# The ten products of each merge stage, each made of seven products of quarters

## The reference, cut to what matters

```python
for l in range(DEPTH):                      # DEPTH = 2
    h = rmsnorm(x, norm_w[l])               # x: 256 x 1024
    proj = h @ w_in[l]
    (..., gate_a, gate_b) = jnp.split(proj, SPLIT_IDX, axis=-1)
    y_a = gated_delta_branch(...)           # 256 x 1024
    y_b = diff_attention_branch(...)        # 256 x 1024
    merged = (jax.nn.sigmoid(gate_a) * (y_a @ w_pa[l])
              + jax.nn.sigmoid(gate_b) * (y_b @ w_pb[l]))
    x = x + merged @ w_out[l]
```

## Time and profile before

| | |
|---|---|
| time, three runs | 2027.78 us median, 2026.0 to 2027.93 |
| profiled execution | 2026.38 us, its span 2024.6 us |
| merge stage of layer 0, first gate product to turning of x | 330.83 to 477.21 us of the span |
| TensorE, VectorE, ScalarE, GpSimd busy | 1957.6, 747.8, 421.5, 100.1 us |

### The profile page before, as it was taken

One profiled execution on the slowest core, in us unless ns is written; L12 is line 12 of the kernel. 1 busy time (PEld: TensorE's weight loads), 2 busy tenths in 40 slices (PEclk: granted clock), 3 DMA queues, 4 the chain that ended last, 5 costly groups with the idle time before them and its releaser, 6 DMA issues.

```text
span 2024.6 us, 26469 instructions
## 1 busy us (share of the span) xinstructions
PE 1957.6 (97%) x10820; PEld 1052.1 (52%) x10820; DVE 747.8 (37%) x2088; ACT 421.5 (21%) x1076; POOL 100.1 (5%) x84
## 2 busy tenths in 40 slices
PE   8999999999999999999999999999999999999997
PEld 7854667886854567884553333333333333333334
DVE  4868675213759676211242122221122112111213
ACT  2261564111061565211131000000000000000003
POOL 0031220000021220000000000000000000000000
PEclk9999999999999999999999999999999999999999
DMA  7634122343643212347659999999999999999992
GB/s 264 252 122 164 46 84 84 126 156 136 226 144 130 84 43 85 125 171 261 227 216 393 428 427 427 429 430 428 431 427 432 430 426 431 429 429 427 428 422 89
DMA packets 99843, 552.29 MB, mean 273 GB/s; under 512 B 8685, under 2 KB 15249, under 8 KB 78738
## 3 DMA queue, kind: packets, MB, share of 16 engines
q1 hardware_dynamic: 99730, 550.66, 67.5%
HBM read 547.43 MB, written 3.21 MB: 272 GB/s over the span
## 4 chain that ended last, share of the span: by engine, by line
PE 81%; DMA 15%; ACT 1%; DVE 1%; SPq 1%; issue 1%; DVEq 0%; ACTq 0%
PE bank L652 29%; DMA region<-w_gate_up_dram 15%; PE bank L1236 14%; PE bank L1268 8%; PE bank L774 6%; PE bank L1010 3%; PE bank L995 3%; PE bank L1179 2%; PE bank L1165 2%; PE bank L1094 1%; PE bank L1223 1%; PE bank L854 1%; PE bank L911 1%; SPq L457 1%; PE bank L878 1%
## 5 line engine op out<-in xcount | busy, mean ns | idle before, releaser
L652 PE MATMUL bank<-region 128*128 128x256 f32 (+2 forms) x2352 | 604.2, 417 | 4.9 <-DVE region L1734 2.6
L652 PEld LDWEIGHTS bank<-region 128*128 128x128 f32 x2352 | 439.8, 190 | 157.9 <-issue 106.5
L1236 PE MATMUL bank<-region 128*64 128x512 f32 x1872 | 416.6, 598 | 22.5 <-DMA region<-w_gate_up_dram 21.6
L1236 PEld LDWEIGHTS bank<-region 128*64 128x64 f32 x1872 | 131.2, 138 | 303.8 <-issue 263.6
L2346 DVE TENSOR_SCALAR region<-bank 128x512 f32<-128x512 f32 x32 | 22.1, 692 | 681.7 <-PE bank L1236 681.7
L1268 PE MATMUL bank<-region 128*64 128x512 f32 x944 | 210.6, 597 | 9.5 <-issue 8.1
L1268 PEld LDWEIGHTS bank<-region 128*64 128x64 f32 x944 | 77.4, 137 | 123.3 <-issue 123.3
L774 PE MATMUL bank<-region 128*128 128x512 f32 x256 | 129.2, 607 | 0.0
L1679 ACT ACTIVATE region<-region 128x512 f32<-128x512 f32 x32 | 20.2, 630 | 512.6 <-DVE region L2346 512.6
L1683 ACT ACTIVATE region<-bank 128x512 f32<-128x512 f32 x32 | 19.1, 597 | 326.9 <-PE bank L1268 326.9
L1840 DVE SCALAR_TENSOR_TENSOR region<-region,layer_mem 128x256 f32<-128x256 f32 x192 | 78.0, 477 | 0.0
(11 more groups left out here) (348 smaller groups left out, 1929.4 us busy)
## 6 DMA issues: line engine op xcount, KB each, us to landing
region<-w_gate_up_dram SPq DMA_DIRECT2D x32, 4096.0 KB, 38.9
region<-w_down_dram SPq DMA_DIRECT2D x59, 2048.0 KB, 34.5
region<-w_gate_up_dram SPq DMA_DIRECT2D x53, 2048.0 KB, 21.6
region<-w_in_dram SPq DMA_DIRECT2D x43, 2048.0 KB, 8.4
layer_mem<-w_gate_up_dram SPq DMA_DIRECT2D x11, 2048.0 KB, 35.4
region<-w_out_dram SPq DMA_DIRECT2D x6, 2048.0 KB, 8.0
layer_mem<-w_down_dram SPq DMA_DIRECT2D x5, 2048.0 KB, 36.4
region<-rows_scratch SPq DMA_DIRECT2D x4, 2048.0 KB, 9.3
```

The source lines that it names most:

```text
L652: mm = pe.matmul(dst, lhs(k), w(k), start=(k == 0), stop=(k == n_k - 1))
L1236: mm = pe.matmul(pb[g][hf * 64:(hf + 1) * 64, :], XT[:, 2 * (j % 2) + kk, j // 2, :], wj[:, kk, c:c + NB], start=(first and j == 0 and kk ...
```

## The change

Each tile's product, 256 positions by 1024 by 512, is cut in two along each side. With the halves of the 1024 rows called k0, k1, of the 512 columns f0, f1, of the positions t0, t1, seven products of quarters (128 positions, 512 rows, 256 columns) take the place of the eight that the plain form has. Sums of quarters stand in for quarters, and results are carried from one quarter of the output to the next:

- GpSimd makes four sums or differences of weight quarters for each tile (`tile_sums`), each 128 partitions by 1024 elements. Three go to memory of their own, one overwrites a quarter of the tile. Tile 0's come behind the diagonal of head 6, tile 1's behind that of head 7, tile 2's and 3's wait for all gating, the later ones for product 6 of two tiles before, and the last of the four for its product 3. Each operation but the third waits for the one that it reads.
- VectorE makes four sums of row quarters (`row_sum`), 128x512 each, for hT (in heads 2 to 5), yaT, ybT and mT.
- TensorE adds up products in PSUM quarters of 256 columns. A product of tiles 0 to 7 is two blocks of 128 features, four matmuls of 128 positions each; in tiles 8 and 9 it is four matmuls of 256 columns. Each ends with a signal of its own, counted in `MERGE_ORDER`.
- ScalarE copies one PSUM quarter into another twice per tile (`upper_right`, `lower_left`), so that TensorE adds on top.
- VectorE takes a tile's quarters out as they get ready (`on_upper`, `lower_right`, then `gate_lower` or `gate_merge`), and keeps the gate's scaling, clamp and multiplication.
- Turned rows of y_a and y_b (and of x from layer 1 on) go to banks 0, 1, 2, 4; products 4 and 3 of tile 1 stand between the turnings and the wait for their copies.
- Slots are freed by product 3 of their tile. The loads of the mixing stage's first tiles wait for product 3 of tiles 0, 1 and 7 of layer 1 instead of all gating.
- Some single signals share a semaphore, two groups of matmuls in the heads (`attention_out`, `chunk_out`) mark their start once per bank, and a fill of zeros is wider.

The core of the diff:

```diff
+        def w_quarter(w, f, kh):
+            return w[:, kh * 4:kh * 4 + 4, f * S:(f + 1) * S]
+        def row_quarter(rows_T, kh, t):
+            return rows_T[:, kh * 4:kh * 4 + 4, t * P:(t + 1) * P]
...
+        MERGE_ORDER = ((1, 0), (5, 0), (2, 0), (6, 0), (1, 1), (7, 0), (2, 1), (5, 1), (6, 1), (4, 0), (3, 0), (7, 1), (4, 1), (3, 1),
+                       (1, 2), (5, 2), (2, 2), (6, 2), *((p, i - (p in (7, 4, 3))) for i in range(3, 8) for p in (1, 5, 7, 2, 6, 4, 3)),
+                       (1, 8), (7, 7), (5, 8), (4, 7), (3, 7), (1, 9), (5, 9), *((p, i) for p in (2, 6, 7, 4, 3) for i in (8, 9)))
...
-            if pos < 24:
-                return "merge_ps1", l * 8 + pos - 15
-            return "xo_ps", l * 4 + pos - 21
+            return "product_ps", products_until(l, 3, pos - 16)
...
+                def quarter(p, i, weights, rows_of, f, t, start=False):
+                    dst = quarter_ps(i, f, t)
+                    if i >= 8:
+                        for k in range(4):
+                            mm = pe.matmul(dst, rows_of[:, k, :], weights[:, k, :], start=(start and k == 0), stop=(k == 3), skip_group_check=True)
+                        mm.then_inc(s("product_ps"), 1)
+                        return
+                    for b in range(2):
+                        for k in range(4):
+                            mm = pe.matmul(dst[:, b, :], weights[:, k, b * P:(b + 1) * P], rows_of[:, k, :],
+                                           start=(start and b == 0 and k == 0), stop=(k == 3), skip_group_check=True)
+                    mm.then_inc(s("product_ps"), 1)
...
+                product_1(0)
+                product_5(0)
                 chunk_state(H - 1)
-                gate_part(0, 0, 0, 1)
+                product_2(0)
+                product_6(0)
                 chunk_ws(H - 1)
-                gate_part(0, 0, 1, 0)
+                product_1(1)
                 chunk_out(H - 1)
+                product_7(0)
+                product_2(1)
+                pe.wait_ge(s("gd_qs"), hb + H)
+                product_5(1)
...
+                transpose16(lambda t, k: ya[:, k, t, :], 3 * l + 1, bank=ROW_BANKS, between=lambda: product_4(1))
                 pe.wait_ge(s("z_gated"), l * 8 + 8)
+                transpose16(blk(qb), 3 * l + 2, bank=ROW_BANKS, between=lambda: product_3(1))
+                product_1(2)
...
+                for i in range(3, 8):
+                    product_1(i)
+                    product_5(i)
+                    product_7(i - 1)
+                    product_2(i)
+                    product_6(i)
+                    product_4(i - 1)
+                    product_3(i - 1)
+                product_1(8)
+                product_7(7)
+                product_5(8)
+                product_4(7)
+                product_3(7)
+                product_1(9)
+                product_5(9)
+                for product_of in (product_2, product_6, product_7, product_4, product_3):
+                    product_of(8)
+                    product_of(9)
...
+                def upper_right(i):
...
+                    act.wait_ge(s("product_ps"), products_until(l, 1, i))
+                    act.activation(quarter_ps(i, 0, 1), quarter_ps(i, 0, 0), ACT.Copy).then_inc(s("quarter_cp"), 1)
...
+                    if 2 <= n < 6:
+                        row_sum(hT, hT_sum, n - 2, 0)
...
+                def lower_right(i):
+                    dve.wait_ge(s("product_ps"), products_until(l, 7, i))
+                    dve.tensor_tensor(right_quarter(i, 1), right_quarter(i, 0), quarter_ps(i, 1, 0), ALU.add).then_inc(s("w_c3"), 1)
...
+                def gate_merge(i):
+                    g, m = i // 4, i % 2
+                    dve.wait_ge(s("product_ps"), products_until(l, 3, i))
+                    dve.wait_ge(s("w_c3"), l * MERGED + i + 1)
+                    in_layer.do(dve.tensor_tensor(gate_quarter(1, m, 0), gate_quarter(1, m, 0), quarter_ps(i, 1, 0), ALU.mult))
+                    dve.tensor_tensor(right_quarter(i, 0), right_quarter(i, 0), quarter_ps(i, 0, 1), ALU.add).then_inc(s("quarter_out"), 1)
+                    dve.wait_ge(s("quarter_out"), quarters_out(l, "lower", i))
+                    for f in range(2):
+                        in_layer.do(dve.tensor_tensor(gate_quarter(f, m, 1), gate_quarter(f, m, 1), right_quarter(i, f), ALU.mult))
...
+                    if m == 1:
+                        for f in range(2):
+                            dve.tensor_tensor(mT[:, 4 * g + 2 * f:4 * g + 2 * f + 2, :], mg[2 * f].rearrange("p (b c) -> p b c", b=2),
+                                              mg[2 * f + 1].rearrange("p (b c) -> p b c", b=2), ALU.add).then_inc(s("merged"), 1)
...
+                gate_clamp(0)
+                copies16(3 * l + 1, lambda k: (yaT[:, k, :], None), ROW_BANKS)
...
+                for n in range(4):
+                    row_sum(yaT, yaT_sum, n, 4)
+                copies16(3 * l + 2, lambda k: (ybT[:, k, :], None), ROW_BANKS)
...
+                def tile_sums(i):
...
+                    pool.wait_ge(s(f"w_in_slot{slot}"), 16 * (k + 1))
+                    pool.tensor_tensor(sums[:, 0], w_quarter(w, 1, 0), w_quarter(w, 1, 1), ALU.add).then_inc(s("w_sum"), 1)
+                    pool.wait_ge(s("w_sum"), 4 * T + 1)
+                    pool.tensor_tensor(sums[:, 1], sums[:, 0], w_quarter(w, 0, 0), ALU.subtract).then_inc(s("w_sum"), 1)
+                    pool.tensor_tensor(w_quarter(w, 1, 0), w_quarter(w, 0, 0), w_quarter(w, 1, 0), ALU.subtract).then_inc(s("w_sum"), 1)
+                    pool.wait_ge(s("w_sum"), 4 * T + 2)
+                    if i >= 4:
+                        pool.wait_ge(s("product_ps"), products_until(l, 3, i - 2))
+                    pool.tensor_tensor(sums[:, 2], w_quarter(w, 0, 1), sums[:, 1], ALU.subtract).then_inc(s("w_sum"), 1)
...
                     diagonal(n)
+                    if n == H - 2:
+                        tile_sums(0)
+                for i in range(1, MERGED):
+                    tile_sums(i)
```

More of the change, by code:

```diff
@@ L712, in _ @@
                         pe.wait_ge(s("const_in"), 16 * 9)
-                        pe.wait_ge(s("rel_wide"), 1)
-                        pe.matmul(pb[4][:, :], rel_wide, bucket, start=True, stop=True).then_inc(s("bias_ps"), 1)
+                        await_once(pe, "rel_wide")
+                        pe.matmul(pb[4][:, :], rel_wide, bucket, start=True, stop=True).then_inc(once("bias_ps"), 1)
                     if u == 2:
@@ L911, in chunk_out @@
                             mm = pe.matmul(pb[7][:, t * P:(t + 1) * P], E_all[:, n, 2 * d + t, :], us[:, 2 * d + t, :],
-                                           start=(d == 0), stop=(d == 1))
+                                           start=(t == 0 and d == 0), stop=(d == 1), skip_group_check=True)
                     mm.then_inc(s("gd_o_ps"), 1)
@@ L2172, in gate_clamp @@
+                def gate_clamp(i):
+                    m = i % 2
+                    dve.wait_ge(s("quarter_out"), quarters_out(l, "lower", i))
+                    for f in range(2):
+                        in_layer.do(dve.tensor_tensor(gate_quarter(f, m, 1), gate_quarter(f, m, 1), rr_rows(1), ALU.mult))
                     in_layer.fence()
-                    for m in range(2):
-                        ins = dve.tensor_scalar(mg[2 * j + m], mg[2 * j + m], -40.0, None, ALU.max)
+                    for f in range(2):
+                        ins = dve.tensor_scalar(mg[2 * f + m], mg[2 * f + m], -40.0, None, ALU.max)
+                        if f == 0:
+                            in_layer.do(ins)
@@ new lines, in _ @@
+                gate_clamp(1)
+                dve.wait_ge(s("tr_act"), 2 * (3 * l + 3))
+                dve.wait_ge(s("tr_dve"), 2 * (3 * l + 3))
+                for n in range(4):
+                    row_sum(ybT, ybT_sum, n, 8)
+                on_upper(2)
+                lower_right(2)
+                on_upper(3)
+                gate_merge(2)
+                lower_right(3)
+                gate_merge(3)
+                dve.wait_ge(s("merged"), 4 * l + 2)
+                on_upper(4)
@@ new lines, in _ @@
+                lower_right(4)
+                row_sum(mT, mT_sum, 0, 12)
+                on_upper(5)
+                gate_lower(4)
+                gate_clamp(4)
+                lower_right(5)
+                on_upper(6)
+                gate_lower(5)
+                gate_clamp(5)
+                lower_right(6)
+                on_upper(7)
+                gate_merge(6)
+                lower_right(7)
+                gate_merge(7)
+                dve.wait_ge(s("merged"), 4 * l + 4)
+                for n in range(1, 4):
+                    row_sum(mT, mT_sum, n, 12)
@@ new lines, in x_quarter, with x_add @@
+                def x_quarter(i, f, t):
+                    c = (i - 8) * NB + f * S
+                    return x[:, t, c:c + S]
+                def x_add(i, f, t, src):
```

(8 more changed lines are left out.)

312 lines of the change are left out of this document (204 added, 108 removed).

## The result

Changed kernel: 2062.15 us median of 4 runs (2060.81 to 2064.43); kernel before on the same chip: 2027.86 us, 4 runs (2026.0 to 2028.35). The ratio is 1.0172, 95% interval 1.0154 to 1.0190: slower by 1.7%, 34.3 us. The forecast was 2047. The profiled execution has a span of 2059.0 us, against 2024.6 of the earlier trace rows.

What follows compares the result with a forecast made beforehand. TensorE's matmul stream bounds the merge. Per layer, 129.3 us of TensorE work plus 26.9 idle from VectorE waiting for GpSimd, less 146.4, gives +9.8; 2026.4 + 2 x 9.8 = 2046.0, stated as 2047 us against the median, range 2003 to 2066.

Steps and rivals of the forecast that it cites:

- likeliest case: Whole kernel: GpSimd's operation takes between 2.3 and 2.5 us, giving 2040 to 2053 us; chance 0.42.
- C: TensorE's clock falls to half pace behind new gaps, 1.8 us lost six times, 11 more: 2058 us; chance 0.15.
- ceiling: Merge: TensorE alone, with some 0.7 us of idle, would save at most 16.4 us per layer, 33 in all.
- Rival D: Merge products: weight loads pace the 128-column matmuls, 71 us more per layer, 2190 us; chance 0.03.
- Items 1 and 2: Heads 6 and 7: VectorE's softmax operations wait for GpSimd's sums, delaying turned probabilities; TensorE loses 6.8 and 6.7 us.
- rival A: Heads 6 and 7: tensor_scalar on one input doesn't wait for GpSimd; +3.7 us per layer, 2035 us; chance 0.15.
- Item 3: After the gating: sums of tiles 2 and 3 delay VectorE's turned-row copies and row sums; losses 2.1 and 4.6 us.
- Item 4: Tiles 3 to 7: VectorE keeps up despite up to two waits a tile; one late addition costs 0.9 us.
- Item 5: Output, before product 2 of tile 8: VectorE's last merge work meets tile 9's sums; loss 5.8 us.
- Edits taken at nothing: Row sums in heads 2 to 5, renamed signals, start flags, banks, wider fills, moved loads: no added time on TensorE's path.
- The stretch named as a sign: Merge, TensorE's first to last product: 149 to 157 us would show the forecast right.
- Rival B: VectorE wins turns against GpSimd, idle under 17 us per layer: -15 to -7 per layer, 2005 us; chance 0.25.

Runs made afterwards that it cites:

- e4_tiny: Changed kernel with all GpSimd sums cut to 32 of 1024 elements; 2936.2 us with other expert rounds, so read only to layer 1's end: layers -15.7 and -15.9 us.
- e8_halves: Changed kernel with each GpSimd sum made in two operations of 512 elements; 2041.16 us, 1.0069 of the kernel before.
- e5_pieces: Changed kernel with each GpSimd sum made in four operations of 256 elements; 2017.19 us, 0.9955 of the kernel before.
- e2_late: Changed kernel with GpSimd's sums for tiles 0 and 1 started only behind VectorE's z_low of heads 6 and 7; 2029.84 us, 1.0014 of the kernel before.
- e7: Changed kernel with sums in four operations of 256 elements and tiles 0 and 1 started behind z_low of heads 6 and 7; 2003.12 us, 0.9883 of before.

## Why the prediction was right, and what it missed

The direction, the mechanism and the places were right; the size was 15 us short. The time lies in the stated range of 2003 to 2066, but outside the 2040 to 2053 of its likeliest case, and near C's 2058, which had a chance of 0.15.

- **Products.** 111 ns per recorded was forecast. Measured: 112 (544 in 61.17 us). The ceiling was 16.4 us per layer with 0.7 of idle, or 16.6 with e4_tiny's 0.46; e4_tiny reaches 15.7 and 15.9, so the matmuls were 0.9 and 0.7 too cheap. Rival D fell.
- **GpSimd's operation.** 2.4 us was forecast; the page has L2689 20 times with a mean of 2404 ns, and the three others lie between 2.39 and 2.48.
- **Items 1 and 2, heads 6 and 7.** 6.8 and 6.7 us forecast, 6.69 to 6.70 measured, four times. Tensor_scalar within SBUF waits like the rest (4.85 us for two), so rival A fell. The sum laid out four VectorE operations there, and five wait: the tensor_scalar of 128x2 before them (L2221) was overlooked. That item 1 came out right all the same is luck in part: GpSimd's burst of four ended the stretch, not VectorE's count; e8_halves, where the burst is longer than the count, is where the same oversight showed.
- **Item 3.** 2.1 and 4.6 forecast; 1.60 and 2.76 in layer 0, 1.59 and 4.64 in layer 1. The first was counted 0.5 too high. The second has two values, by phase, and the forecast's is the longer one.
- **Item 4.** 0.9 forecast; 0.48 in layer 0, nothing in layer 1.
- **Item 5.** 5.8 forecast; 5.91 and 6.36.
- **Edits taken at nothing.** Right: up to head 6 the two traces run 0.2 us apart (305.71 and 305.94), so the row sums of heads 2 to 5 cost nothing, and no weight load ended a wait of TensorE in the merge.
- **The stretch named as a sign.** 149 to 157 us from first to last product was given; it is 144.0 in layer 0 (348.19 to 492.20) and 148.6 in layer 1. The waits of heads 6 and 7 stand before the first product, so half of the forecast's idle did not belong to this stretch; the sum itself counted it rightly.
- **Idle in sum.** 26.9 forecast, 24.1 and 26.0 measured. Rival B needed less than 17 and did not come; its mechanism had to be built (e5_pieces has 7.0 us of idle in layer 0). Its threshold was too mild besides: e8_halves has 14.4 us of idle in layer 0 (4.60 + 4.61 + 2.01 + 3.13) and is slower than before by 5.7 there, again by the pace.
- **The step that failed: the pace behind the gaps.** The forecast of 2047 took the gaps at their bare length and left the lowered clock to rival C, with 0.15. It happened. Against e4_tiny, which has neither, layer 0 of the changed kernel is 186.5 - 155.6 = 30.9 us longer, of which 24.1 - 0.5 = 23.6 are idle: 7.3 us of lower pace. Layer 1: 35.7 - 25.5 = 10.2. Together 17.4 (before rounding), against 11 in C and nothing in the forecast. Nearly all of it can be placed: 4.2 us in heads 6 and 7 of layer 0 (the first product at 348.19 comes 17.6 later than in the earlier trace rows, counted from the mask, and 13.4 of that are idle), 4.1 in those of layer 1 (from the turning of x to the first product 338.4 us instead of 320.9, 13.4 of it idle), 2.0 and 3.0 us in the 80 products behind the last gap (19.45 and 20.48 for what takes 17.5 in e5_pieces), and 2.3 in the 624 of layer 1 (72.23 against 69.92). The remaining 1.8 is not placed; part of it is that the brackets are short (L941 of head 6 moved by 6.85 us where its bracket says 6.69).

So 2 x 9.8 = 19.6 forecast, less 3.7 of idle over-counted, plus 17.4 of pace and 1.6 of matmuls, is 34.9; the traces show 35.0. C had the place right and the size nearly: it took the three long gaps per layer at 1.8 us each, from the first stretch of the program; measured, the six cost 1.4, 2.4 and 2.0 in layer 0 and 2.6, 1.3 and 3.0 in layer 1, 12.7 together against 11. The Trainium skill (TensorE: Matmul & The Clock Gate, Why this matters for your kernels) says that idle gaps between bursts bring the slower clock back. The runs agree, with 0.53 against 1.00 in the window from 340 to 345. No row of the kernel before had such a gap in mid-run, and I let that absence speak against C, when the only stretch behind a wait of that length spoke for it; it should have been a term of the sum, and the forecast 2058.

## What to carry to other kernels

Before work is given to an engine that stands idle, look at what the other engines do in the same microseconds. GpSimd's long elementwise operations cost VectorE about one of their own length for each two-input operation or tensor_scalar within SBUF, up to the end of the burst. Two remedies worked here without touching the arithmetic: cut the operations short, and start them where VectorE waits or reads PSUM; together they turned +1.7% into -1.2%. And when TensorE gets new gaps, put the pace behind them into the sum: here gaps of 4.6 to 6.9 us cost 1.3 to 3.0 us each besides their length, and gaps of 2.0 to 3.1 us either 1.4 to 2.1 or next to nothing.

## What the runs showed of the hardware

- VectorE's tensor_scalar within SBUF waits for a GpSimd operation, even on 128x2 elements (1.06 us against 0.23 in e2_late). The Trainium skill (SBUF — State Buffer, Who interferes with whom) lists tensor_scalar at double rate among those that take the shared pair; the trace agrees, 4.85 us for two against 0.61.
- GpSimd hardly slows while VectorE waits: 2.34 to 2.39 us in head 6. Beside VectorE's row sums in the merge it reaches 2.81 (at 394.84). A VectorE operation with one input in PSUM does not wait for it (0.58 us for two in e2_late against 0.59).
- GpSimd's 128x256 takes 0.69 us alone (16 in 11.12 in e7), so quarters cost 2.8 us per sum instead of 2.4, and still gain.
- The lowered clock can cost about the same behind a gap of 2.0 us as behind one of 6.7 (2.1 and 2.35 us, head 7 of layer 0). But not every short gap lowers it: behind 2.02 us in head 6 of layer 1 of e5_pieces the clock stayed at 1.00, behind the 3.13 us before product 2 of tile 8 in e8_halves the 80 products took 17.50 us, full pace, and behind 2.30 us in the changed kernel the 544 products took 61.17, 112 ns each. What tells these apart is not settled; no run varied the length of one gap alone.
